# Gate and decay rows of a gated delta layer earlier, and weight splits between the steps of two half tiles

## The chip, the cores and the metric

The kernel runs on one core of a Trainium2 chip, in one launch. The metric is the device time of the whole program in microseconds (us), the median of several runs.

## What is computed

Two blocks of a network over 272 tokens (16 meta tokens and 256 real ones) and then 256 tokens, width 1024, all in f32. Block one has four layers: two with forgetting attention, one gated linear attention (GLA), one gated delta network (GDN), each followed by a SwiGLU. Block two has two layers of its own kind. The change touches only the mixer of the GDN layer:

```python
proj = h @ w_in
qkv, gate, a, beta_logit = jnp.split(proj, [...])
qkv = jax.nn.silu(causal_depthwise_conv(qkv, conv_w))      # 4 taps
q = l2norm(q) * (GDN_DK ** -0.5)                           # k likewise, v not
beta = jax.nn.sigmoid(beta_logit)
g = -jnp.exp(a_log) * jax.nn.softplus(a + dt_bias)
o = chunked_scan(gdn_chunk, state0, (q, k, v, g, beta), GDN_CHUNK)
o = rmsnorm(o, o_gain) * jax.nn.silu(gate)
return o @ w_out
```

`gdn_chunk` takes 64 tokens: it needs exp of the running sums of `g` (the decays), products of keys with keys and queries, a triangular solve, and a state of 128 x 128 for each of 8 heads.

## The kernel before

**Tiles.** The projection of the GDN layer is cut into 32 tiles of 128 output features (`GDN_TILES`: tiles 0 to 7 are keys, 8 to 15 queries, 16 to 23 values, 24 to 31 the gate). A tile is 24 matmuls of 272 columns: 8 chunks of the input width, three products each, since every f32 operand is split into a high and a low part. Tiles are written to two banks of PSUM in turn, so TensorE can't start tile t+2 before VectorE has evacuated tile t (`evacuated`).

**Weights.** They stream in blocks of four tiles, in two halves, into a ring of four slots (SyncE issues the loads). A half goes through ScalarE, which writes the rounded high part (`split` in the scalar program, line 1492 writes `ring_hi`), and then VectorE, which writes the low part (`split` in the vector program, line 2027 writes `ring_lo`). In the GDN stage both come out of `hooks`: after(t), or before(t) on ScalarE, splits half 0 of the next block at t = 0, 4, 8 ... and half 1 at t = 2, 6, 10 ... So a half that is split at tile t is first used by tile t+4.

**Half tiles.** All other work of the GDN mixer is laid into the projection by hand. `gdn_steps` gives each step a half: half 2t is the middle of tile t, half 2t+1 its end. TensorE carries out its part of half 2t after 12 of the 24 matmuls of tile t, and its part of half 2t+1 after the last (`at_half`). The other engines run through their parts in program order, and every step waits on semaphores for its inputs. Where a step needs TensorE, then VectorE or ScalarE, then TensorE, the last part stands one or more halves later.

**VectorE, tile t.** `at_half(2t-1)`, `at_half(2t)`, the evacuation of tile t (line 2575), the taps of tile t-1 (`taps`, lines 2546, 2549, 2551), and `after(t)`, the split. Before the halves come, at t = 3, `logits()` (the raw gate rows), at t = 5 `sums()` (running sums), at t = 7 `decays()` (copies into the rows that are spread later).

**ScalarE, tile t.** `at_half(2t-1)`, `at_half(2t)`, the first tap of tile t (`conv_first`), `before(t)`, the split, and `silu(t-1)`: the silu of tile t-1 and, for keys and queries, its square into one of three `raw` buffers. TensorE sums the square over features (`stat`); `("stat", i)` stands at half 7, 9, 11, 13, 15 for i = 0 to 4 and at 16, 18, 20 for 5 to 7, each in TensorE's program order between the tiles. ScalarE also runs `forget_rows()` at t = 4 (sigmoids, a logarithm and an exponential, between `logits()` and `sums()`) and `decay_rows()` at t = 6 (two exponentials, between `sums()` and `decays()`). Its functions live in tables: sigmoid, silu and the pair logarithm/exponential are three of them in this program, and a change of table is an instruction of its own (ACT_TABLE_LOAD).

**The raw gate rows** come from 48 narrow matmuls that TensorE runs right after tile 0 (`narrow`, `ab_ready`). Their first reader across halves is `("tokens",)` at half 23, with `key_refine` at half 21 before it.

Of the kernel before, what the change touches and what calls it, by code (L numbers as in the profile page):

```python
# [75 lines left out]
GDN_TILES = [(part, h) for part in "kqvg" for h in range(NH)]  # L76
# [200 lines left out]
def build(nc, wt, xin, memin, params, consts, smallw, rpb, out):  # L277
    ctx = ExitStack()
    with ctx:
# [56 lines left out]
        def pcol(name, i=0):  # L336
            off, _ = PARAMS[name]
            return par[:, off + i:off + i + 1]

        def const(name):  # L340
            off, n = CONSTS[name]
            return con[:, off:off + n]
# [205 lines left out]
        def acc(tile, width, m=P, banks=BANKS):  # L548
            return ps[0:m, tile % banks, 0:width]
# [10 lines left out]
        def hooks(split, n, tpb, fine):  # L560

            def at(t):
                g = n.block + t // tpb + 1
                if g < len(half_width):
                    if not fine:
                        if t % tpb == 0:
                            split(g, 0)
                        if t % tpb == tpb // 2:
                            split(g, 1)
                    elif t % (tpb // 4) == 0:  # L570
                        quarter = t % tpb // (tpb // 4)
                        split(g, quarter // 2, part=quarter % 2)
            return at
# [907 lines left out]
        def _(act):  # L1481
# [9 lines left out]
            def fn(dst, src, f, **kw):  # L1491
                return nc.scalar.activation(dst, src, f, **kw)  # L1492

            def ln_exp():

                nc.scalar.preload_act_table_set("natural_log_exp_and_others")
# [233 lines left out]
            def gdn(before):  # L1730
                def forget_rows():
                    act.wait_ge(f_ready, n.logit + 1)
                    step(fn(n_rows[0:NH, 3, :], n_rows[0:NH, 2, :], ACT.Abs))
                    fn(n_rows[0:NH, 4, :], n_rows[0:NH, 4, :], ACT.Sigmoid)
                    step(fn(n_rows[0:NH, 3, :], n_rows[0:NH, 3, :], ACT.Sigmoid))
                    ln_exp()
                    fn(n_rows[0:NH, 3, :], n_rows[0:NH, 3, :], ACT.Ln)
                    fn(gain8[0:NH, :], pcol("gdn_alog")[0:NH, :], ACT.Exp).then_inc(fl_ready, 1)

                def decay_rows():  # L1740
                    act.wait_ge(rows_ready, 1)
                    fn(n_rows[0:NH, 2, 0:SEQ], n_rows[0:NH, 2, 0:SEQ], ACT.Exp)
                    fn(n_rows[0:NH, 3, :], n_rows[0:NH, 0, :], ACT.Exp).then_inc(kdec_ready, 1)
# [70 lines left out]
                def at_half(p):  # L1814
                    for name, *which in steps[p]:
                        if name in acts:
                            acts[name](*which)

                def silu(t):
                    part, h = GDN_TILES[t]  # L1820
                    act.wait_ge(conv_last, n.conv + t + 1)
                    a = n_qkv[:, GDN_PLACE[part] + h, :]
                    fn(a, a, ACT.Silu).then_inc(conv_silu, 1)
                    if t < 2 * NH:
                        if t >= 3:
                            act.wait_ge(gstat_ready, t - 2)
                        act.wait_ge(conv_silu, n.conv + t + 1)
                        fn(raw[:, t % 3, :], a, ACT.Square).then_inc(gsq_ready, 1)

                for t, (part, h) in enumerate(GDN_TILES):  # L1830
                    if t == 4:
                        forget_rows()
                    if t == 6:
                        decay_rows()
                    if t:
                        at_half(2 * t - 1)
                    at_half(2 * t)
                    act.wait_ge(evacuated, BANKS + n.tile + t + 1)
                    if part == "g":
                        before(t)  # L1840
                        if t == 24:
                            silu(t - 1)
                        if h in (3, 7):
                            a = n_gate[:, h - 3:h + 1, :]
                            fn(a, a, ACT.Silu).then_inc(silu_gate, 4)
                            ln_exp()
                    else:
                        fn(n_cc[:, t % 2, :], n_cp[:, t % 2, 0:T], ACT.Copy, scale=pcol("gdn_conv", 4 * (GDN_PLACE[part] + h))).then_inc(conv_first, 1)
                        before(t)
                        if t:  # L1850
                            silu(t - 1)
                for p in range(2 * len(GDN_TILES) - 1, GDN_END + 1):
                    at_half(p)
                n.logit += 1
# [153 lines left out]
        def _(v):  # L2008
# [8 lines left out]
            def step(ins):  # L2017

                mark(ins)
                v.wait_ge(dve_step, steps[0])  # L2020
# [328 lines left out]
            def gdn(after):  # L2349
                R = lambda i: n_rows[0:NH, i, :]  # L2350

                def logits():
                    v.wait_ge(ab_ready, 1)
                    V.memset(n_rows[:, 0:2, :], 0.0)
                    V.tensor_tensor(R(4), ps[0:NH, 5, 0:T], rstd[0:NH, :], ALU.mult)
                    step(V.tensor_tensor(R(3), ps[0:NH, 6, 0:T], rstd[0:NH, :], ALU.mult))
                    V.tensor_scalar(R(2), R(3), pcol("gdn_dt")[0:NH, :], None, ALU.add).then_inc(f_ready, 1)

                def sums():
                    v.wait_ge(fl_ready, n.logit + 1)  # L2360
                    step(V.scalar_tensor_tensor(out=R(2), in0=R(2), scalar=0.0, in1=R(3), op0=ALU.max, op1=ALU.subtract))
                    step(V.tensor_scalar(R(2), R(2), gain8[0:NH, :], -1.0, ALU.mult, ALU.mult))
                    step(V.tensor_tensor_scan(R(0), const("gdn_reset")[0:NH, :], R(2), 0.0, ALU.mult, ALU.add))
                    b = R(0)[:, 0:SEQ].rearrange("p (c t) -> p c t", t=64)
                    V.tensor_tensor(R(2)[:, 0:SEQ].rearrange("p (c t) -> p c t", t=64), b[:, :, 63:64].broadcast_to([NH, 4, 64]), b, ALU.subtract)
                    V.tensor_copy(n_rows[32:32 + NH, 0, :], R(4)).then_inc(rows_ready, 1)

                def decays():
                    v.wait_ge(kdec_ready, 1)
                    V.tensor_copy(n_rows[96:96 + NH, 0, 0:SEQ], R(2)[:, 0:SEQ])  # L2370
                    ends = R(3)[:, 0:SEQ].rearrange("p (o c t) -> p o c t", o=1, t=64)[:, :, :, 63].broadcast_to([NH, NH, 4])
                    eye = ident[0:NH, 0:NH].rearrange("p (h o) -> p h o", o=1).broadcast_to([NH, NH, 4])
                    V.tensor_tensor(R(4)[:, 0:32].rearrange("p (h c) -> p h c", c=4), ends, eye, ALU.mult).then_inc(rows_ready, 1)
# [161 lines left out]
                def at_half(p):  # L2535
                    for name, *which in order[p]:
                        if name in acts:
                            acts[name](*which)
# [15 lines left out]
                new_rstd(T)  # L2554
                step(V.memset(n_cp[:, :, 0:3], 0.0))
                for t, (part, h) in enumerate(GDN_TILES):
                    if t == 3:
                        logits()
                    if t == 5:
                        sums()  # L2560
                    if t == 7:
                        decays()
                    if t:
                        at_half(2 * t - 1)
                    at_half(2 * t)
                    v.wait_ge(acc_ready, n.tile + t + 1)
                    if part == "g":
                        if h in (0, 3):
                            v.wait_ge(wt_ready, 1 + h // 3)
                        dst = n_gate[:, h, :]  # L2570
                    else:
                        if t >= 2:
                            v.wait_ge(conv_last, n.conv + t - 1)
                        dst = n_cp[:, t % 2, 3:3 + T]
                    V.tensor_tensor(dst, acc(n.tile + t, T, P, 2), rstd[:, :], ALU.mult).then_inc(evacuated, 1)  # L2575
                    if 0 < t <= 24:
                        taps(t - 1)
                    after(t)
                for p in range(2 * len(GDN_TILES) - 1, GDN_END + 1):
                    at_half(p)  # L2580
                n.conv += 24
# [176 lines left out]
            for name, nb, tpb, kc in plan:  # L2758
                after = hooks(split, n, tpb, name.startswith(("in2_", "memkv")))
# [308 lines left out]
```

## Time and profile before

| | us |
|---|---|
| median of 3 runs | 2431.13 |
| the runs | 2427.98 to 2431.22 |
| the profiled execution | 2425.49 |
| its span, first to last instruction | 2423.9 |

| engine | busy us | share of the span |
|---|---|---|
| TensorE, matmuls | 2268.8 | 94% |
| TensorE, weight loads | 2157.7 | 89% |
| VectorE | 1555.5 | 64% |
| ScalarE | 1207.1 | 50% |
| GpSimd | 611.7 | 25% |

PE is TensorE, PEld its weight loads, DVE VectorE, ACT ScalarE, POOL GpSimd. The GDN projection and mixer run from 782.6 to 1039.5 us of the span. A line of the profile such as L763 is a helper that issues all matmuls, L1492 one that issues all of ScalarE's functions; there the tile's name or the time tells them apart. The clock in the rows is the granted clock of TensorE as a share of 2.4 GHz: 1.00 is 2.4 GHz and 0.50 is 1.2 GHz, and a value between is a mean over a stretch with both.

### The profile page before, as it was taken

What the parts mean: (1) busy time and instruction counts of PE and PEld (TensorE: products, weight loads), DVE (VectorE), ACT (ScalarE), POOL (GpSimd) and SP (SyncE); (2) the same over time, 40 slices, a digit from 0 to 9 for tenths busy, and PEclk for the clock granted to TensorE, in tenths of its full rate; (3) what the DMA queues carried; (4) which work ended last, traced back from release to release, by engine and by line L of the source; (5) the groups of instructions that cost most, each with busy time, mean ns of one, the idle gap of its engine ahead of it and who ended that gap; (6) DMA issues with size and microseconds to landing.
All of it is one profiled execution on the core that took longest, in us unless ns stands there. A gap on an engine that the chain in (4) does not pass through costs nothing.

```text
span 2423.9 us, 48151 instructions
## 1 busy us (share of the span) xinstructions
PE 2268.8 (94%) x19050; PEld 2157.7 (89%) x19050; DVE 1555.5 (64%) x2520; ACT 1207.1 (50%) x1861; POOL 611.7 (25%) x738
## 2 busy tenths in 40 slices
PE   4999999999999899989998999998999999899998
PEld 4878999899999778789997889997798998788998
DVE  4665654746554675466556665657767976767994
ACT  4555444544544642355445555544556654456653
POOL 3113211013211020031111132115234534123540
PEclk9999999999999999999999999999999999999999
DMA  4324545424546312135453235555353555343554
GB/s 168 104 89 139 174 157 181 150 87 135 177 153 196 100 59 67 43 137 173 159 189 96 97 117 181 183 176 186 105 188 131 181 169 175 97 137 132 183 167 137
DMA packets 52863, 344.03 MB, mean 142 GB/s; under 512 B 5904, under 2 KB 7120, under 8 KB 20176
## 3 DMA queue, kind: packets, MB, share of 16 engines
q1 hardware_dynamic: 51984, 336.26, 42.0%
q0 software_dynamic: 704, 5.31, 0.5%
q8 instruction: 125, 2.05, 0.3%
q14 instruction: 50, 0.41, 0.1%
HBM read 340.43 MB, written 1.05 MB: 141 GB/s over the span
## 4 chain that ended last, share of the span: by engine, by line
PE 72%; DVE 11%; ACT 8%; issue 5%; DMA 1%; POOL 1%; DVEq 0%; ACTq 0%; SPq 0%
PE ps L763 70%; ACT ring_hi L1492 3%; DVE ring_lo L2027 3%; ACT arena L1492 3%; ACT hrs L1492 1%; DVE newt L2044 1%; DVE hrs L2045 1%; DVE newt L2043 1%; DVE arena L2136 1%; PE ps L952 1%; ACT sq L1492 1%; POOL arena L2903 0%; DMA ring<-in 0%; ACT L1492 0%; DMA ring<-out 0%
## 5 line engine op out<-in xcount | busy, mean ns | idle before, releaser
L763 PE MATMUL ps<-arena_r,ring_hi 128*128 128x272 f32 (+1 forms) x6688 | 1592.1, 287 | 13.1 <-DVE arena L2164 5.4
L763 PEld LDWEIGHTS ps<-arena_r,ring_hi 128*128 128x128 f32 x6688 | 1167.7, 191 | 21.1 <-issue 7.3
L763 PE MATMUL ps<-y_r,ring_hi 128*128 128x272 f32 (+1 forms) x3424 | 1014.1, 296 | 38.0 <-DVE ring_lo L2027 23.7
L2027 DVE TENSOR_TENSOR ring_lo<-ring,ring_hi 128x2048 fp32r<-128x2048 f32 (+2 forms) x372 | 740.8, 1992 | 387.8 <-ACT ring_hi L1492 385.9
L763 PE MATMUL ps<-y_r,ring_lo 128*128 128x272 f32 (+1 forms) x3424 | 982.9, 287 | 0.0
L763 PEld LDWEIGHTS ps<-y_r,ring_hi 128*128 128x128 f32 x3424 | 655.4, 191 | 62.2 <-issue 37.7
L1492 ACT ACTIVATE ring_hi<-ring 128x2048 fp32r<-128x2048 f32 (+2 forms) x372 | 611.8, 1647 | 117.5 <-DMA ring<-dn 48.6
L763 PEld LDWEIGHTS ps<-y_r,ring_lo 128*128 128x128 f32 x3424 | 657.4, 192 | 0.0
L763 PE MATMUL ps<-arena_r,ring_lo 128*128 128x256 f32 (+1 forms) x1632 | 465.2, 285 | 0.0
L763 PEld LDWEIGHTS ps<-arena_r,ring_lo 128*128 128x128 f32 x1632 | 309.4, 190 | 0.0
L1492 ACT ACTIVATE arena<-arena 128x272 f32<-128x272 f32 (+7 forms) x200 | 93.2, 469 | 381.1 <-DVE arena L2597 262.6
L2895 POOL CAST arena_r<-arena 128x272 fp32r<-128x272 f32 (+1 forms) x132 | 134.7, 1021 | 539.8 <-DVE arena L2599 417.8
L763 PE MATMUL ps<-arena 64*64 64x64 f32 (+18 forms) x2792 | 216.5, 265 | 39.7 <-ACT arena L1492 16.1
L763 PEld LDWEIGHTS ps<-arena 64*64 64x64 f32 (+10 forms) x2792 | 157.4, 145 | 80.6 <-issue 45.1
L2903 POOL TENSOR_SCALAR arena<-x,par 128x272 f32<-128x272 f32 (+1 forms) x98 | 92.7, 946 | 332.3 <-ACT y_r L1492 331.4
L1492 ACT ACTIVATE sq<-x 128x256 f32<-128x256 f32 (+1 forms) x120 | 50.3, 419 | 191.6 <-DVE x L2073 191.3
L1492 ACT ACTIVATE arena<-ps 128x256 f32<-128x256 f32 (+7 forms) x291 | 91.0, 364 | 61.8 <-PE ps L763 36.4
L2896 POOL TENSOR_TENSOR arena_r<-arena,arena_r 128x272 fp32r<-128x272 f32 (+1 forms) x132 | 102.4, 776 | 10.6
L2073 DVE TENSOR_TENSOR x<-ps,x 128x256 f32<-128x256 f32 (+1 forms) x112 | 48.1, 430 | 86.4 <-PE ps L763 85.8
L2887 POOL CAST arena_r<-arena 128x256 fp32r<-128x256 f32 (+1 forms) x40 | 21.7, 542 | 313.9 <-DVE arena L2697 144.7
L1492 ACT ACTIVATE arena<-arena,par 128x256 f32<-128x256 f32 (+1 forms) x112 | 62.6, 583 | 75.5 <-DVE arena L2575 54.0
L2638 DVE SCALAR_TENSOR_TENSOR arena<-arena,par 128x256 f32<-128x256 f32 x176 | 99.5, 623 | 0.0
(234 smaller groups left out, 1711.5 us busy)
## 6 DMA issues: line engine op xcount, KB each, us to landing
ring<-gu SPq DMA_DIRECT2D x88, 1024.0 KB, 5.1
ring<-dn SPq DMA_DIRECT2D x64, 704.0 KB, 4.0
ring<-up SPq DMA_DIRECT2D x44, 1024.0 KB, 5.1
ring<-fox_in SPq DMA_DIRECT2D x32, 1024.0 KB, 5.1
ring<-sdn SPq DMA_DIRECT2D x32, 704.0 KB, 4.1
ring<-gdn_in SPq DMA_DIRECT2D x16, 1024.0 KB, 5.1
ring<-in SPq DMA_DIRECT2D x16, 1024.0 KB, 5.1
ring<-gla_in SPq DMA_DIRECT2D x12, 1024.0 KB, 5.1
```

Of the source, the lines that this page charges most:

```text
L763: return nc.tensor.matmul(dst, w, mv, start=start, stop=stop)
L952: last = nc.tensor.transpose(ps[0:w, 4 + u % 2, q * P:q * P + un["qn"]], un["p"][0:un["qn"], a:a + w], ident[0:un["qn"], 0:un["qn"]])
L1492: return nc.scalar.activation(dst, src, f, **kw)
L2027: V.tensor_tensor(ring_lo[:, slot, cols], ring[:, slot, cols], ring_hi[:, slot, cols].bitcast(F32), ALU.subtract).then_inc(lo_ready, 2 if ...
L2043: step(V.scalar_tensor_tensor(out=a, in0=square_sum, scalar=size * EPS, in1=r, op0=ALU.add, op1=ALU.mult))
L2044: step(V.scalar_tensor_tensor(out=b, in0=a, scalar=-0.5 / size, in1=r, op0=ALU.mult, op1=ALU.mult))
L2045: step(V.scalar_tensor_tensor(out=r, in0=b, scalar=1.5, in1=r, op0=ALU.add, op1=ALU.mult))
L2073: V.tensor_tensor(dst[:, c, :], take(c, width), dst[:, c, :], ALU.add).then_inc(evacuated, 1)
L2638: V.scalar_tensor_tensor(out=u_cc[:, q, :], in0=u_gp[:, q, 1 + tap:1 + tap + SEQ], scalar=par[:, bass.ds(i * 24 + (w0 + 12 * b + 3 * q + 1 ...
L2895: step(G.tensor_copy(hi_r[:, c, :], lo[:, c, :]))
L2896: G.tensor_tensor(lo_r[:, c, :], lo[:, c, :], hi_r[:, c, :].bitcast(F32), ALU.subtract).then_inc(h_split, 1)
L2903: step(G.tensor_scalar(lo[:, c, :], src[:, c, :], pcol(gain, c), 1.0, ALU.mult, ALU.mult))
```

## The change

On ScalarE `forget_rows()` moves from tile 4 to tile 1 and `decay_rows()` from tile 6 to tile 2. `silu(0)` is no longer run in tile 1: tile 2 runs `silu(0)` and `silu(1)`, and from tile 3 on all is as before. On VectorE `logits()` moves from tile 3 to tile 1, `sums()` from 5 to 2, `decays()` from 7 to 3. Apart from that, `after(t)`, the split, moves from the end of tile t to tile t+1, between `at_half(2t+1)` and `at_half(2t+2)`. TensorE's and SyncE's programs are unchanged, and no computation is added or removed.

```diff
-                    if t == 4:
+                    if t == 1:
                         forget_rows()
-                    if t == 6:
+                    if t == 2:
                         decay_rows()
                     if t:
                         at_half(2 * t - 1)
...
                         before(t)
-                        if t:
-                            silu(t - 1)
+                        for done in ([], [], [0, 1])[t] if t < 3 else [t - 1]:
+                            silu(done)
...
                 for t, (part, h) in enumerate(GDN_TILES):
+                    if t == 1:
+                        logits()
+                    if t == 2:
+                        sums()
                     if t == 3:
-                        logits()
-                    if t == 5:
-                        sums()
-                    if t == 7:
                         decays()
                     if t:
                         at_half(2 * t - 1)
+                        after(t - 1)
                     at_half(2 * t)
...
                     if 0 < t <= 24:
                         taps(t - 1)
-                    after(t)
+                after(len(GDN_TILES) - 1)
```

## Rows read from the trace of the kernel before

**Rows 1.** Waits of TensorE, 774 to 1045 us: us in total, times, longest.
```profile
PE ps L763 <- ACT raw L1492: 4.9, 2, 4.0
PE ps L763 <- DVE arena L2429: 4.8, 1, 4.8
...
PE ps L763 <- DVE arena L2479: 3.8, 2, 2.6
PE ps L763 <- DVE arena L2444: 3.4, 1, 3.4
...
PE ps L763 <- DVE arena L2384: 3.1, 1, 3.1
PE ps L763 <- DVE arena L2461: 2.0, 1, 2.0
PE ps L763 <- DVE arena L2575: 1.8, 1, 1.8
```

**Rows 2.** Busy time by stretch: stretch, length, PE, PEld, DVE, ACT, POOL; clock, DMA.
```profile
774.66:1039.50 264.84, 232.73 (x2835) 203.48 (x2833) 160.16 (x274) 117.47 (x203) 25.76 (x24) 0.91 0.23 77
...
819.94:826.31 6.37, 6.37 (x27) 5.59 (x27) 3.21 (x7) 5.29 (x8) 0.00 (x0) 0.53 0.00 0
849.00:857.00 8.00, 8.00 (x55) 6.54 (x52) 4.48 (x13) 4.04 (x7) 0.00 (x0) 0.57 0.03 9
863.00:867.00 4.00, 4.00 (x18) 2.85 (x18) 3.90 (x7) 0.22 (x1) 1.45 (x1) 0.57 0.23 43
907.00:915.00 8.00, 5.50 (x74) 5.24 (x76) 4.13 (x11) 0.83 (x3) 0.12 (x1) 0.57 0.14 25
...
982.00:987.00 5.00, 5.00 (x38) 4.55 (x35) 0.64 (x3) 1.26 (x2) 0.00 (x0) 0.66 0.08 13
```

**Rows 3.** Timeline of TensorE: start, us, instruction; tile 1 begins, and `stat` 0.
```profile
792.60 0.29 PE L763 MATMUL ps<-y_r,ring_hi 128*128 128x272 f32 x1
...
801.69 0.62 PE L763 MATMUL ps<-raw,con 128*8 128x272 f32 x2
```

**Rows 4.** Timeline of VectorE around `logits()`, `sums()` and the evacuations that follow.
```profile
804.07 0.51 DVE L2354 MEMSET arena<- 128x544 f32 x1
...
805.52 0.42 DVE L2575 TENSOR_TENSOR arena<-ps,rstd 128x272 f32<-128x272 f32 x1
...
807.53 0.44 DVE L2575 TENSOR_TENSOR arena<-ps,rstd 128x272 f32<-128x272 f32 x1
...
817.10 0.42 DVE L2361 SCALAR_TENSOR_TENSOR arena<-arena 8x272 f32<-8x272 f32 x1
...
819.44 0.44 DVE L2575 TENSOR_TENSOR arena<-ps,rstd 128x272 f32<-128x272 f32 x1
```

**Rows 5.** Timeline of ScalarE: `forget_rows()`, first tap and silu of the tile, `decay_rows()`.
```profile
808.26 0.41 ACT L1492 ACTIVATE arena<-arena 8x272 f32<-8x272 f32 x1
...
812.48 0.51 ACT L1492 ACTIVATE arena<-arena,par 128x272 f32<-128x272 f32 x1
...
814.81 1.28 ACT L1492 ACT_TABLE_LOAD   x1
816.10 0.43 ACT L1492 ACTIVATE arena<-arena 128x272 f32<-128x272 f32 x1
816.62 0.43 ACT L1492 ACTIVATE raw<-arena 128x272 f32<-128x272 f32 x1
...
823.66 0.74 ACT L1492 ACTIVATE arena<-arena 8x256 f32<-8x256 f32 x2
```

**Rows 6.** The chain that ended last, around the split of tile 18: start, us.
```profile
899.50 0.45 DVE arena L2575
...
902.39 2.29 DVE ring_lo L2027
...
909.50 0.92 PE ps L763 x10
```

**Rows 7.** Timeline of VectorE around the split of tile 30.
```profile
1017.84 2.29 DVE L2027 TENSOR_TENSOR ring_lo<-ring,ring_hi 128x2048 fp32r<-128x2048 f32 x1 [2.09 <-ACT ring_hi L1492]
```

## Prediction, written before the change was run

> **What bounds the kernel now.** I first read the busy shares: TensorE is busy for 94% of the span, so an edit pays only where TensorE waits or runs slowly. Then the stretch of the GDN stage: in 264.8 us TensorE's matmuls are busy for 232.7, so 32.1 us are idle, and the mean granted clock is 0.91 [rows 2]. The waits of TensorE say what ends the idle time [rows 1]. 4.9 us (one wait of 4.0, one of 0.9) end with a square in `raw`, 1.8 with an evacuation, 3.1 with L2384 (`key_refine`), 4.8 with L2429 (`xy`), 3.4 with L2444 (`keys`), 2.0 with L2461 (`queries`), 3.8 with L2479 (`state`, two waits, of 2.6 and 1.2). Together 23.8 us. What is left, about 8 us, is the tail of the stage, which the change doesn't touch.
>
> Each long wait is followed by a stretch at 1.2 GHz. What that costs, if TensorE is busy in it, is length times (1 - mean clock), since the low part runs at half speed: tile 7 6.37 x 0.47 = 3.0, and some 0.5 for the `stat` before it; after the wait of 3.1, 8 x 0.43 = 3.4; after the 4.8, 3.4 less the idle share, 2.6; after the 2.0, 5 x 0.34 = 1.7 [rows 2]. Two stretches like the last follow the 3.4 and the 2.6. Sum 3.5 + 3.4 + 2.6 + 3 x 1.7 = 14.6. Not every such stretch needs a wait: at 863 to 867 TensorE is busy throughout, with narrow matmuls before, and still 1.7 is lost [rows 2].
>
> **Part 1, the rows earlier.** Removed: the waits of 4.9 and 1.8, because `forget_rows()` in tile 4 puts a sigmoid, a logarithm and two table changes ahead of the silu of tile 3, and `sums()` holds the evacuation of tile 5 (817.10 to 819.44) [rows 4, 5]. With their low clock that is 6.7 + 3.5 = 10.2.
>
> Added: the same chain now runs against `stat` 0. I replay it with durations from the rows. The narrow matmuls end at 792.6 [rows 3]. `logits()` takes 805.52 - 804.07 = 1.5 [rows 4]: 794.1. `forget_rows()` takes 812.48 - 808.26 = 4.2 [rows 5]: 798.3, plus about 0.1 for each hand-over: 798.6. `sums()` takes 819.44 - 817.10 = 2.3 [rows 4]: 801.0. The exponentials of `decay_rows()`, whose table is in place, 0.7 [rows 5]: 801.7. Then ScalarE runs the first tap of tile 2, the high half of the weights, the table for silu, `silu(0)` and its square, as it did from 812.48 to 816.62 + 0.43, 4.6 [rows 5]: 806.3. TensorE's program has `stat` 0 between tiles 3 and 4, where it now arrives at 801.7 without waiting [rows 3]. So it waits 4.6 us where it waited for nothing. That is the length of waits that cost 2.6 to 3.5 in clock above; I take 3.0. Added 7.6, net gain of part 1: 2.6.
>
> What is queued behind: on VectorE `sums()` waits for ScalarE, and the evacuation of tile 2 comes after it, at 801.0; TensorE needs that for tile 4, after `stat` 0, so the same wait hides it. The evacuation of tile 1 waits for `logits()` and the split of tile 0 (794.1 + 2.3 = 796.4) and is needed for tile 3 at 792.6 + 2 x 3.03 = 798.7 (three tiles took 801.69 - 792.60 [rows 3]). After 806.3 a tile and its `stat` give TensorE 3.0 + 0.6 = 3.6 us; VectorE needs 2.0 a tile for evacuation and taps (807.53 - 805.52 [rows 4]) and 2.3 every second tile, ScalarE 1.4 and 1.9 every second tile. Both catch up, so `stat` 1 to 5 don't wait. Three of six early table loads fall away (3 x 1.28 of ScalarE), which counts only in this catching up.
>
> The Trainium skill ("ScalarE: Activation LUTs", section What ACT_TABLE_LOAD costs) gives a change of table 1.28 us plus a drain of 1.38. The trace disagrees on the drain: the load at 814.81 ends at 816.09 and silu starts at 816.10 [rows 5]. By the page the new wait would be 3 x 1.38 = 4.1 longer; the sum without it stands.
>
> **Part 2, the splits between the steps.** A split takes 2.3 on VectorE and before that waits for ScalarE's high part, which starts only after the evacuation. Now the steps of half 2t-1 come first. The pattern is the split of tile 18: evacuation 899.50, taps to about 901.5, split 902.39 to 904.68, then the refining of the query roots and `xy`, on which TensorE waits until 909.50 [rows 6]. Without the split ahead the steps start at 901.5, 3.2 earlier; I take 3.4 off the 4.8, with bounds 2.5 and 4.8, since GpSimd runs beside them.
> - L2384: `key_refine` can run before the split of tile 10; its own time, 1.7, then hides behind TensorE's last half of tile 11. All 3.1 goes.
> - L2444: the split of tile 24 goes behind `keys` 4. Of 3.4 some 0.3 stays: 3.1.
> - L2461 and L2479: gate tiles have no taps, so VectorE idles 2.1 and splits for 2.3 before the steps [rows 7] whose inputs TensorE has had ready since early in that time. 2.0 + 3.8 go.
> Sum 3.4 + 3.1 + 3.1 + 2.0 + 3.8 = 15.4.
>
> What is late next: a split now waits for the steps' inputs, and half 2t and the evacuation of tile t wait for it. Its weights are used by tile t+3 at the earliest, some 9 us on, so that is free. TensorE's part of half 2t comes 1.5 us after the end of the tile; a split of 2.3 can make its VectorE part late by 0.8. There are nine tiles with VectorE steps there (11, 17, 19, 21, 23, 25, 27, 29, 31); bounds 0 and 9 x 0.8 = 7.2. I take 1, since the results of half 2t are used at the next half or later.
>
> Clock: 3.4 + 2.6 + 5.1 = 11.1 hang on the waits of part 2. After the key stage the narrow matmuls alone may keep 1.7, and of the other 7.7 I take two thirds: 1.7 + 5.1 = 6.8, bounds 2 and 11.
>
> **Sum.** 2.6 + 15.4 - 1.0 + 6.8 = 23.8 against the profiled execution's 2425.5 (span 2423.9 and 1.6 around it): 2401.7. The median of the runs shown is 5.6 above that execution, so I forecast 2431.1 - 23.8 = 2407.3. Bounds: the waits give 2.6 + 14.5 - 7.2 = 9.9 at least and 19.4 at most, clock 2 to 11: a gain of 12 to 30.
>
> **Rivals.**
> - *Part 1 costs more.* The squares stay late after `stat` 0: `stat` 1 and 2 wait too, 2 us each, and the low clock lasts as in the old stretch, 3 us more. 7 us: 2414. Against it: the two engines need less a tile than TensorE. For it: both are nearly full from 805 to 848.
> - *The waits only move.* What waited at the end of a tile waits half a tile later, behind the same split; the 15.4 and their clock stay and only 2.6 is gained: 2428.5, no change. Against it: the chains named end in a step of an end half, with the split right before it.
> - *Slower.* All nine splits land on TensorE's path, 2.3 each, and each also pulls the clock down (1.7 each): 9 x 4.0 = 36 is lost. Part 1's 2.6 and part 2's 15.4 and 6.8 are still gained: 36 - 24.8 = 11 slower, 2442. It decides from where a step of half 2t is needed by TensorE within 2.3 us of the tile's end. For it: it is TensorE's normal pattern that a result is wanted a half later (1.5 us). Against: the evacuations have a whole tile of slack.
> - *Table changes with their drain*, as above: 4.1 more wait, 2411. The row speaks against it.
> That the change doesn't do what it says is ruled out: every engine's order is its program order.
>
> **How the numbers follow.** As replayed 0.74 (2407), part 1 costlier 0.12 (2414), waits move 0.07 (2428), slower 0.04 (2442), drain 0.01 (2411), more gain than the bounds 0.02. Faster by over 0.2%, which is about what a measurement of this kernel can tell from no change, 0.74 + 0.12 + 0.01 + 0.02 = 0.89; within 0.2% 0.07; slower 0.04. The range leaves out the last two cases: 2400 to 2421.
>
> **What would show it.** TensorE waits 4 to 5 us for `raw` near 802, followed by a clock of 0.50 until about 812, and no wait of 4.0 near 813 nor of 1.8 near 818. `stat` 5 finds its square ready. Waits on L2384 and L2461 are gone, that on L2429 is under 2, on L2444 under 1. The mean clock of the stage rises from 0.91 to about 0.94, and the stage ends some 24 us earlier, with its idle time down from 32 to about 15. I am wrong if waits on the steps of middle halves (L2415, L2508, evacuations) have come in, or if the low clock stays without waits.

## The result and the profile after

| | before | after |
|---|---|---|
| median, us | 2431.18 | 2404.07 |
| range of 4 runs | 2427.98 to 2437.72 | 2399.78 to 2405.76 |
| profiled execution / its span | 2425.49 / 2423.9 | 2404.67 / 2403.0 |

The ratio of the runs is 0.9871, with a 95% interval of 0.9851 to 0.9891: the change is worth 22 to 36 us, with 31.4 in the middle. The two medians of the table alone differ by 27.1, which lies in that interval. On the 2431.1 of the forecast that is 2399.8, just under the lower end of its range of 2400 to 2421, and 7.5 under the forecast of 2407.3; the median of 2404.07 itself lies inside the range. A second measurement gave 0.9872 (0.9851 to 0.9894). Direction and mechanism were right. A size was not.

TensorE's waits in the changed kernel, from 774 to 1025 us (us in total, times, longest), answer to [rows 1]:

```profile
PE ps L763 <- ACT raw L1492: 4.7, 1, 4.7
PE ps L1295 <- DVE arena L2493: 4.3, 1, 4.3
PE ps L763 <- DVE arena_r L2528: 3.2, 1, 3.2
PE ps L763 <- DVE arena L2429: 0.9, 1, 0.9
PE ps L1198 <- DVE arena L2446: 0.8, 1, 0.8
PE ps L763 <- DVE arena L2444: 0.2, 1, 0.2
```

The second and third are the tail of the stage, which was there before, and so was the 0.8. Of the waits of [rows 1] those on L2384, L2461, L2479 and on the evacuation are gone, that on L2429 fell from 4.8 to 0.9 and that on L2444 from 3.4 to 0.2. New is one wait of 4.7 for a square.

The stage, from the first load of its weights to the first load of the next layer's, and stretches of it, answer to [rows 2] (stretch, length, PE, PEld, DVE, ACT, POOL; clock, DMA). After:

```profile
772.38:1021.55 249.17, 235.12 (x2917) 208.11 (x2916) 165.77 (x278) 115.65 (x203) 28.06 (x26) 0.95 0.26 86
807.00:814.00 7.00, 5.82 (x23) 4.92 (x24) 3.08 (x5) 3.11 (x8) 0.00 (x0) 0.51 0.14 60
848.00:852.00 4.00, 4.00 (x22) 4.00 (x21) 3.09 (x9) 3.74 (x5) 0.00 (x0) 0.57 0.05 18
858.00:862.00 4.00, 4.00 (x18) 2.85 (x17) 3.90 (x8) 0.19 (x1) 2.07 (x2) 0.57 0.49 133
862.00:1008.00 146.00, 140.50 (x2178) 125.38 (x2176) 98.19 (x170) 58.80 (x126) 21.18 (x20) 1.00 0.21 70
```

Before, over the same bounds:

```profile
770.50:1047.95 277.45, 245.34 (x2917) 216.09 (x2916) 164.60 (x278) 119.61 (x206) 27.34 (x25) 0.91 0.23 77
```

The stage is 28.3 us shorter. The same 2917 matmul records stand in both rows, so the second number separates the two effects: the idle time fell from 277.45 - 245.34 = 32.1 to 249.17 - 235.12 = 14.1, by 18.1, and the busy time by 10.2, which I put down to the clock, since the work is the same. For 146 us, from the rest of the key stage to the tail, the granted clock is now 1.00, full speed (2.4 GHz). ScalarE's records fell from 206 to 203: the three table loads.

The new wait can be followed through the changed kernel's timelines. VectorE:

```profile
794.71 0.51 DVE L2354 MEMSET arena<- 128x544 f32 x1 [3.12 <-PE ps L763]
...
800.63 0.43 DVE L2361 SCALAR_TENSOR_TENSOR arena<-arena 8x272 f32<-8x272 f32 x1 [0.37 <-ACT gain L1492]
...
802.98 0.44 DVE L2576 TENSOR_TENSOR arena<-ps,rstd 128x272 f32<-128x272 f32 x1
```

ScalarE:

```profile
796.26 0.43 ACT L1492 ACTIVATE arena<-arena 8x272 f32<-8x272 f32 x1 [2.31 <-DVE arena L2357]
...
800.50 0.51 ACT L1492 ACTIVATE arena<-arena,par 128x272 f32<-128x272 f32 x1
802.98 0.74 ACT L1492 ACTIVATE arena<-arena 8x256 f32<-8x256 f32 x2 [1.96 <-DVE arena L2366]
803.62 0.51 ACT L1492 ACTIVATE arena<-arena,par 128x272 f32<-128x272 f32 x1
804.03 1.89 ACT L1492 ACTIVATE ring_hi<-ring 128x2048 fp32r<-128x2048 f32 x1
805.94 1.28 ACT L1492 ACT_TABLE_LOAD   x1
807.24 0.43 ACT L1492 ACTIVATE arena<-arena 128x272 f32<-128x272 f32 x1
807.70 0.43 ACT L1492 ACTIVATE raw<-arena 128x272 f32<-128x272 f32 x1
```

and TensorE:

```profile
808.18 1.08 PE L763 MATMUL ps<-raw,con 128*8 128x272 f32 x2 [4.66 <-ACT raw L1492]
```

`logits()` starts at 794.71, `forget_rows()` at 796.26, `sums()` at 800.63, `decay_rows()` at 802.98, then come the first tap, the high half, the table for silu, silu and square, and TensorE has waited 4.66 us. The replay in the prediction had the same order and 4.6. Its chain from the end of the narrow matmuls to the square was 806.3 - 792.6 = 13.7; here it is 808.13 - 794.71 = 13.4.

How the waits on the steps went shows at the split of tile 18 (VectorE, the changed kernel; compare [rows 6]):

```profile
893.80 0.44 DVE L2576 TENSOR_TENSOR arena<-ps,rstd 128x272 f32<-128x272 f32 x1 [0.41 <-PE ps L763]
...
895.76 0.43 DVE L2377 SCALAR_TENSOR_TENSOR newt<-ps,arena 8x272 f32<-8x272 f32 x1
...
899.58 0.21 DVE L2429 TENSOR_TENSOR arena<-arena,ps 128x64 f32<-128x64 f32 x1
899.72 2.66 DVE L2027 TENSOR_TENSOR ring_lo<-ring,ring_hi 128x2048 fp32r<-128x2048 f32 x1
```

Evacuation to refining is 2.0 us now and was 5.2 (899.50 to 904.7), and the split follows the steps. It takes 2.66 instead of 2.29, and TensorE doesn't wait for it.

### The profile page after: what moved, and what is told of

Its sections match the earlier page's. It is cut to its first block, busy times and chain, and to the rows that moved or that the text cites. A ratio compares the mean times of both kernels' runs of the same rounds, so it can differ in the third digit from the quotient of the medians.

```text
span 2403.0 us, 48146 instructions
## 1 busy us (share of the span) xinstructions
PE 2263.0 (94%) x19050; PEld 2154.7 (90%) x19050; DVE 1556.0 (65%) x2520; ACT 1203.6 (50%) x1858; POOL 610.4 (25%) x738
## 4 chain that ended last, share of the span: by engine, by line
PE 76%; DVE 9%; ACT 7%; issue 4%; DMA 2%; POOL 1%; DVEq 0%; ACTq 0%; SPq 0%; POOLq 0%
PE ps L763 74%; ACT ring_hi L1492 2%; ACT arena L1492 2%; DVE ring_lo L2027 2%; ACT hrs L1492 1%; DVE newt L2044 1%; PE ps L952 1%; DVE hrs L2045 1%; DVE newt L2043 1%; DVE arena L2136 0%; ACT sq L1492 0%; POOL arena L2904 0%; DMA ring<-gla_in 0%; DMA arena<-arena 0%; DMA ring<-in 0%
## 5 line engine op out<-in xcount | busy, mean ns | idle before, releaser
L763 PE MATMUL ps<-y_r,ring_hi 128*128 128x272 f32 (+1 forms) x3424 | 1014.0, 296 | 35.8 <-DVE ring_lo L2027 23.8
L1492 ACT ACTIVATE arena<-ps 128x256 f32<-128x256 f32 (+7 forms) x291 | 90.4, 362 | 49.4 <-PE ps L763 23.8
```

Source lines behind the costliest of these rows:

```text
L763: return nc.tensor.matmul(dst, w, mv, start=start, stop=stop)
```

## The experiments

All stage numbers below are from one profiled execution of each kernel, over the same bounds; the ratios are those of the runs to the kernel before.

| kernel | stage, us | busy | idle | ratio, 95% interval |
|---|---|---|---|---|
| before | 277.45 | 245.34 | 32.1 | |
| before, second and third profile | 277.41, 281.81 | 245.42, 248.20 | 32.0, 33.6 | |
| changed | 249.17 | 235.12 | 14.1 | 0.9871 (0.9851 to 0.9891) |
| changed, again | 247.83 | 233.68 | 14.2 | 0.9872 (0.9851 to 0.9894) |
| rows only | 281.00 | 248.67 | 32.3 | 0.9981 (0.9967 to 0.9996) |
| rows only, again | 280.52 | 249.45 | 31.1 | 0.9991 (0.9979 to 1.0004) |
| splits only | 252.70 | 237.00 | 15.7 | 0.9880 (0.9866 to 0.9894) |
| changed, splits of 24 to 30 back | 266.81 | 243.98 | 22.8 | 0.9939 (0.9928 to 0.9951) |
| changed, split of 18 back | 254.28 | 234.79 | 19.5 | 0.9874 (0.9853 to 0.9896) |
| changed, split of 24 back | 260.60 | 242.27 | 18.3 | 0.9902 (0.9881 to 0.9923) |
| changed, sums of squares later | 242.22 | 232.55 | 9.7 | 0.9838 (0.9826 to 0.9851) |

**Which part carries it.** Rows early, splits at the end of the tile (shown against the changed kernel):

```diff
                     if t:
                         at_half(2 * t - 1)
-                        after(t - 1)
...
                         taps(t - 1)
-                after(len(GDN_TILES) - 1)
+                    after(t)
```

> Gate and decay rows in tiles 1 to 3, but every split at the end of its tile, as before. Theory A (the gain is that of the moved splits; moving the rows trades one wait for another): the wait of 4.7 us for the square of tile 0 comes in, those of 4.0, 1.8 and 0.9 between 805 and 830 go, the waits on L2384, L2429, L2444, L2461 and L2479 stay, and the time is 2 to 5 us under the kernel before. Theory B (the rows carry at least a third of the 28 us, because ScalarE and VectorE are nearly full in the early tiles): 9 us or more under it.

The ratio, 0.9981, is 1 to 8 us faster; the stage is 3.6 us longer. The late waits are all there, as theory A has it (that on L2384 is 2.6 instead of 3.1, that on L2444 3.1 instead of 3.4), but the wait for the first square is 6.4, not 4.7. VectorE's timeline of this kernel tells why:

```profile
794.64 2.29 DVE L2027 TENSOR_TENSOR ring_lo<-ring,ring_hi 128x2048 fp32r<-128x2048 f32 x1 [2.46 <-ACT ring_hi L1492]
796.99 0.51 DVE L2354 MEMSET arena<- 128x544 f32 x1
```

With the old order the split of tile 0 stands ahead of `logits()`, which starts when the split is through. In the changed kernel `logits()` goes first. So the second part of the change makes the first 1.7 us cheaper. Since run time and stage had different signs, the kernel was measured again.

> Rows early and splits at the end of their tile, once more. Open: the runs came out 1 to 8 us under the kernel before, the stage of the profiled execution 3.6 us over it. By the waits alone it is level (24.9 against 24.6). Theory A: both are the clock's scatter and moving the rows alone is worth nothing; the stage is 275 to 282 us (277.5 before) and the ratio between 0.998 and 1.002. Theory B: the rows alone gain; ratio under 0.998 again and a stage under 275.

The ratio was 0.9991 and the stage 280.5, inside what theory A allowed. Theory B is out both times, with its 9 us or more and with its stage under 275. Whether the rows alone are worth 0 or a few us stays open: the second measurement says from 5 faster to 1 slower, both stages are 3 longer than two of before's three and level with its third, and the parts outside the stage scatter more than that (the next layer's mixer alone took 191.5 to 197.3 us over the profiles of this document, from the first load of its weights to the first of the next layer's).

Splits between the steps, rows as before:

```diff
-                    if t == 1:
+                    if t == 4:
                         forget_rows()
-                    if t == 2:
+                    if t == 6:
                         decay_rows()
...
-                    if t == 1:
+                    if t == 3:
                         logits()
-                    if t == 2:
+                    if t == 5:
                         sums()
-                    if t == 3:
+                    if t == 7:
                         decays()
```

(and `silu(t - 1)` in every tile, as before)

> Splits between the steps of the two halves, but the rows in tiles 3 to 7 as before. Theory A: the wait of 4.0 us for the square of tile 3 stays; the one of 1.8 for the evacuation of tile 5 goes, since the running sums no longer stand behind the split of tile 4; the waits on L2384, L2444, L2461 and L2479 are gone and that on L2429 is under 1.5. About 25 to 30 us under the kernel before, so level with the changed kernel within 3 us. Theory B: 9 us or more slower than the changed kernel.

0.9880 is 29 us, level with the changed kernel, and the stage is 24.8 shorter than before. TensorE's waits (774 to 1025 us; the tail's two left out):

```profile
PE ps L763 <- ACT raw L1492: 5.1, 2, 3.0
...
PE ps L763 <- ACT arena L1492: 1.2, 1, 1.2
PE ps L763 <- DVE arena L2429: 0.9, 1, 0.9
```

The wait of 1.8 for the evacuation is gone, as expected. The two for a square were 4.0 and 0.9 and are 3.0 and 2.1, and a wait of 1.2 for a copy of ScalarE is new (more on it below). The stage is 3.5 to 4.9 us longer than in the two profiles of the changed kernel. That the early rows are worth this on top of the moved splits is not shown: two profiles of the kernel before differ by 4.4, and the runs don't tell the two kernels apart.

One thing in this profile speaks against a clock that falls only behind waits. TensorE's last wait before this stretch was 0.2 us, at 947.6, and it is busy throughout:

```profile
952.00:953.00 1.00, 1.00 (x12) 0.69 (x10) 0.00 (x0) 0.00 (x0) 0.00 (x0) 1.00 0.67 106
953.00:954.00 1.00, 1.00 (x22) 0.85 (x18) 0.29 (x1) 0.00 (x0) 0.00 (x0) 0.77 0.78 279
954.00:955.00 1.00, 1.00 (x7) 0.93 (x6) 1.00 (x3) 0.00 (x0) 0.00 (x0) 0.50 1.04 434
955.00:956.00 1.00, 1.00 (x6) 0.96 (x5) 0.52 (x2) 0.00 (x0) 0.79 (x1) 0.50 0.55 229
```

From 953 to 957 the mean clock is 0.57, so 1.7 us are lost. Just before stand 32 narrow matmuls with 8-row operands (951.3 to 953.7), the same kind as before the stretch at 863 to 867 of [rows 2]. In both profiles of the changed kernel these matmuls follow on the same work, with the same 0.2 of waiting before them, and no such stretch comes.

**What a wait costs in clock.** The splits of the last four blocks back at the end of their tiles:

```diff
                         at_half(2 * t - 1)
-                        after(t - 1)
+                        if t - 1 < 24:
+                            after(t - 1)
...
                         taps(t - 1)
-                after(len(GDN_TILES) - 1)
+                    if t >= 24:
+                        after(t)
```

> The changed kernel, with the splits of tiles 24, 26, 28 and 30 back at the end of their tile. The waits on L2444 (3.4), L2461 (2.0) and L2479 (1.2 and 2.6) come back, together 8.9 over the changed kernel. Theory A (low clock comes with the waits): three or four stretches at 0.50 also come back, 1.7 us each, one of them behind the queries, where TensorE never waited: 14 to 16 us slower than the changed kernel in the stage. Theory C (the low clock is set by what TensorE computes, not by waits): 9 us slower.

Slower than the changed kernel by 17.6 in the stage, and by 0.9939 - 0.9871 = 0.7% (16.5 us) in the runs. The idle time grew by 8.8, as both theories say. The busy time grew by 8.9, so theory C as put, with no loss beyond the waits, falls, and theory A was too low on the clock: it gave 5 to 7. Behind the wait on L2444, which ended at 947.1, TensorE ran at 1.2 GHz for nearly 14 us without a pause:

```profile
948.00:963.00 15.00, 15.00 (x92) 12.65 (x89) 2.55 (x5) 0.89 (x4) 2.25 (x2) 0.54 0.22 71
```

In the changed kernel this work (the second half of the weights, the queries, the first values) lies within 946 to 961, with more behind it (139 matmul records against 92), and has no low clock at all:

```profile
946.00:961.00 15.00, 15.00 (x139) 13.31 (x138) 7.67 (x12) 3.88 (x9) 2.26 (x2) 1.00 0.22 71
```

Next, one split at a time. Tile 18 (the kernel for tile 24 has 24 in both places):

```diff
                         at_half(2 * t - 1)
-                        after(t - 1)
+                        if t - 1 != 18:
+                            after(t - 1)
...
                         taps(t - 1)
+                    if t == 18:
+                        after(t)
                 after(len(GDN_TILES) - 1)
```

> The changed kernel, with the split of tile 18 alone back at the end of its tile, so that query_refine and xy stand behind it. Its wait grows from 0.9 to 4.8. Theory A: a stretch at 0.50 follows, as before the change (2.6 us lost), and the stage is 6.5 us longer than that of the changed kernel. Theory C (the low clock is set by what TensorE computes): 3.9 longer.

The wait came back at 4.8, and behind it the low clock (0.51). Two of TensorE's waits:

```profile
PE ps L763 <- DVE arena L2429: 4.8, 1, 4.8
PE ps L763 <- ACT arena L1492: 1.4, 1, 1.4
```

and the stretch behind the first:

```profile
903.00:910.00 7.00, 5.79 (x74) 5.53 (x76) 2.92 (x8) 1.12 (x4) 0.38 (x1) 0.51 0.17 36
```

The stage is 5.1 us longer than the changed kernel's first profile and 6.4 longer than its second, between the two theories. But the idle time grew by 5.4, of which 1.4 is another wait, for a copy of ScalarE, that no theory had; the busy time changed by -0.3 to +1.1, because the stretch at 858 to 862 didn't fall this time.

The two belong together. Seven of the twelve profiles have a low stretch like that one, soon behind 32 narrow matmuls (between 851 and 869, by the profile), and none of these has the wait for the copy some 15 us later: both of the changed kernel, two of before, rows only again, the splits of 24 to 30 back, the sums of squares later. The other five lack the stretch, and all have the wait, of 1.2 to 1.4 us: splits only, the first of rows only, both single splits, the third of before. Two kernels are in both groups, so this varies between executions and need not come from the edit: 1.7 us of low clock are exchanged for 1.4 of waiting. That TensorE waits because it comes there earlier at full clock fits, but no run isolates it. With the exchange taken off both theories, A gives 6.2 and C 3.6. The measured 5.1 to 6.4 is nearer to A, though the scatter of the stage is as large as the difference, and the runs show no cost at all (0.9874).

> The changed kernel, with the split of tile 24 alone back at the end of its tile, ahead of the last keys. The wait on L2444 grows from 0.2 to 3.1. Theory A: the low clock comes back, and with it the stretch behind the queries, where TensorE doesn't wait (1.7 to 6.8 us lost, the latter if it stays low from one to the other): the stage is 4.6 to 9.7 us longer. Theory C: 2.9 longer.

The stage is 11.4 to 12.8 longer, more than A's upper end. The idle time grew by 4.2 (2.9 for this wait, 1.4 for the same copy, which again comes with that stretch missing), the busy time by 7.2 to 8.6. One wait of 3.1 us is followed by this:

```profile
949.00:953.00 4.00, 4.00 (x30) 3.71 (x30) 0.06 (x1) 0.89 (x4) 0.00 (x0) 0.58 0.00 0
956.00:974.00 18.00, 18.00 (x80) 15.76 (x78) 6.85 (x11) 1.91 (x1) 2.26 (x2) 0.53 0.07 30
```

For 18 us TensorE is busy all the time, mostly at 1.2 GHz: 18 x 0.47 = 8.5 lost. In this execution 3 us of waiting at this place go with a stage that is 11 to 13 longer. In the runs it is 0.3% (7 us).

**Why runs and profile differ.** The changed kernel again, and the kernel before twice more:

> The changed kernel once more, timed beside the kernel before. What is open: the time of the first runs (1.3% under before, 22 to 36 us) and the GDN stage of the profiled executions (28.3 us shorter). Theory A (waits and low clock of the stage are the whole effect, the rest of the program scatters by itself): the ratio comes out between 0.987 and 0.990 and the stage within 2 us of 249.2 (from the first load of gdn_in to the first of the next gu). Theory E (something outside the stage also got faster): a ratio of 0.9865 or less.

> The kernel before, once more, for a second profile. Open: by the runs the change is worth about 31 us, by the GDN stage of the profiled executions 28.3 to 29.6. The profiled execution of before (2425.5) was faster than every timed run of it. Theory F (it had a mild clock): behind the waits on L2444 and L2461 TensorE stays at 0.50 from one wait to the next, as it did from 956 to 974 in the kernel with the split of tile 24 alone put back, so that 7 to 9 us are lost there instead of 5.1; the stage is 279 to 284 us long. Theory G (before's stage is always 277.5 and the difference lies outside the stage): 276.5 to 278.5.

> The kernel before, for a third profile, with the same two theories: F, a stage of 279 to 284 us with 7 to 9 us lost to the clock between 962 and 987; G, 276.5 to 278.5. If the two come out differently, the clock behind these waits is drawn anew in each execution, and the 2.0 us between the two come from there.

The changed kernel gave 0.9872 and a stage of 247.8, both as theory A has them. The 0.9865 of theory E was not reached, but the interval doesn't exclude it. Of the two profiles of before one matches the first (277.4, theory G's figure), the other has a stage of 281.8 with the same late waits and

```profile
962.00:976.00 14.00, 14.00 (x91) 11.86 (x88) 2.55 (x5) 0.89 (x4) 2.25 (x2) 0.51 0.22 76
```

which is 14 x 0.49 = 6.9 lost, where the first profile lost 1.7 + 1.7 in two short stretches with full speed between. So F describes one execution and G two: how long the clock stays low behind these waits differs between executions of the same kernel. Over 17 runs of before beside the repeat the mean granted clock of the span was 0.969 to 0.976, and the execution that I read, 0.976, is at the top of that; the changed kernel's four were 0.977 to 0.979.

What the runs gained and the profiles didn't show stays open. As wholes, the profiled executions differ by less than their stages: before's spans are 2423.9, 2424.0 and 2425.0, the changed kernel's 2403.0 and 2404.7, so 19 to 22 us. Outside the stage (span less stage) before took 2143.2 to 2146.6 and the changed kernel 2153.8 and 2156.9. No part of the program out there is changed, and three variants of the changed kernel (splits of 24 to 30 back, split of 24 back, sums of squares later) took 2146.6 to 2146.9, and the other variants lie between, so I read the 7 to 14 us as scatter between executions. How the 27 to 31 us of the runs divide between the stage and the rest is not shown, since only the profiled executions have a trace.

**A faster version.** The added wait can be taken out. Nothing reads the sums of squares before half 20, and with three `raw` buffers the first may wait until half 10. The edit also puts tile 3's evacuation and taps ahead of a split; the two were not run apart.

```diff
-        steps[2 * (i + 3) + (i % NH < 5)].append(("stat", i))
+        steps[(10, 11, 12, 13)[i] if i < 4 else 2 * (i + 3) + (i % NH < 5)].append(("stat", i))
...
                         at_half(2 * t - 1)
-                        after(t - 1)
+                        if t != 3:
+                            after(t - 1)
...
                         taps(t - 1)
+                    if t == 3:
+                        after(2)
                 after(len(GDN_TILES) - 1)
```

> The changed kernel, with the sums of squares of tiles 0 to 3 at halves 10, 11, 12 and 13 instead of 7, 9, 11 and 13, and in tile 3 the evacuation and taps ahead of the split of tile 2. Theory A: the wait of 4.7 for the square of tile 0 and the low clock behind it (2.9) go, other waits stay as in the changed kernel: 6 to 8 us under it. Theory D (the rows' chain is the bound of the early tiles and the wait only moves, to the evacuation of tile 3 or 4 or to a later square): level with the changed kernel within 2 us.

Median 2393.91, ratio 0.9838: 36 to 42 us under before, some 8 under the changed kernel, as theory A has it; theory D is out. The stage is 7.0 and 5.6 shorter than in the two profiles of the changed kernel, its waits are 0.2 (a square), 0.9, 0.8 and 0.2 and the tail, and the 40 us in which the rows are made have TensorE busy and at full speed:

```profile
800.00:840.00 40.00, 39.76 (x354) 33.15 (x354) 32.81 (x56) 28.01 (x45) 0.00 (x0) 1.00 0.40 135
```

## Why the prediction was right in kind and short in size

- **Part 1, the waits.** 6.7 removed and 4.6 added, forecast; 6.7 and 4.7 measured. The chain through `forget_rows()`, `sums()` and the silu table was right to 0.3 us.
- **Part 1, the clock.** 3.5 before, 3.0 forecast, 2.9 measured (5.82 busy at about half speed from 807 to 814). Net gain 2.6 forecast, 2.6 measured inside the changed kernel. Not seen: the two parts aren't independent. Alone the first waits 1.7 longer, because its `logits()` stands behind a split, and the second alone already removes the 1.8.
- **Part 2, the waits.** 15.4 less 1.0 for new delays forecast. Measured 3.9 + 3.1 + 3.2 + 2.0 + 3.8 = 16.0. The 3.4 taken for `xy` was 0.5 short, since GpSimd didn't get in the way (L2377 to L2393 take 2.5 us, not 3.1), and no step of a middle half came late: the allowance of 1.0 was not used. Idle time was forecast at about 15 and is 14.1: it fell by 18.1, where the sum had 2.1 + 14.4 = 16.5, so 1.6 of the shortfall is here.
- **Part 2, the clock: the step that failed.** Forecast 6.8, bounds 2 to 11. Measured in the first two profiles: 10.2 of busy time in all, 0.6 of it part 1's and about 0.6 lost again in the tail, so about 10 (with the changed kernel's second profile 11.7 in all). With part 1's 0.6 against a forecast of 0.5, this term was about 3 us too small, and with the 1.6 above it makes up the 4.5 between the 23.8 of the forecast and the 28.3 of the stage. Two errors are in it. The stretch behind the queries (969 to 973 before, 1.7 lost), which has no wait of its own, was left out of the sum; it went with the others. And the two thirds for the rest had no row behind it; in the changed kernel everything went, while in the kernel with the splits alone one stretch of 1.7 was still there, so that some allowance wasn't wrong. If the runs have the same idle time as the profiles and nothing else differs, 31.4 less 18.1 leaves 13 for the clock (4 to 18 with the interval of the runs); no trace shows that.
- **The basis.** The loss to be regained was read from one execution. Of two more, one has the same busy time in the stage (245.4) and one 2.9 more (248.2), and the one read had a clock of 0.976, at the top of before's runs. The sum was scaled to the median by adding 5.6 on both sides, that is, as if before's extra 5.6 stayed after the change. Part of it may have been low clock behind waits that the change removes. This is argued from the third profile and the clocks of the runs, and not isolated by a run of its own; the spans of the profiled executions, 19 to 22 apart, don't show it.
- **The range.** Its lower end came from adding up the bounds, 30 us, and the clock's bound of 11 was the sum of the stretches of that one execution, not a bound on what they can be. With the 6.9 of the third profile in place of 3.4 the lower end would have been near 2397.
- **The rivals.** "The waits only move": 0.9 and 0.2 stayed where they were, none moved. "Slower", with splits on TensorE's path: no wait of that kind. "Part 1 costs more": `stat` 1 to 5 don't wait. Table changes with a drain: the split of the high half ends at 805.92, the load runs from 805.94 to 807.22 and silu starts at 807.24, so no.

## What to carry to other kernels

Where one engine's long housekeeping step (here 2.3 us behind a wait of about 2 us for another engine) has tiles of slack and short steps have none, put the short ones first at each hand-over; here nothing then waited for the long one. A wait of TensorE can cost more than its length: here the stage grew by one to three times the added idle time (5.1 for 5.4, 17.6 for 8.8, 11.4 for 4.2), so take the clock's share from several executions and bound it widely. A chain moved earlier needs its own slack: move the consumers in TensorE's order with it.

## What the runs showed of the hardware

A stretch at 1.2 GHz doesn't end when TensorE is busy again. With the split of tile 24 put back, a wait of 3.1 us was followed by 18 us with a mean clock of 0.53 in which TensorE never paused; among its matmuls there, besides the full tiles, are those of the queries and scales, whose operands have 8 rows. In the changed kernel, where no such wait went before them, the same instructions ran at 1.00. And the extent varies between executions of one kernel: 3.4 us or 6.9 lost in before's profiles, behind the same waits.

Waits are not the whole of it. Behind the wait on L2444 the clock fell in all seven profiles that have it at 3.1 or 3.4 us. Of the five without it, four stay at 1.00 there, and one, the kernel with the splits alone, falls to 1.2 GHz between 953 and 957, behind 32 narrow matmuls, with TensorE busy throughout. The same kind of stretch between 851 and 869, also soon behind 32 such matmuls and with TensorE busy throughout, came in seven of twelve profiles. What decides between them stays open.
